# Rotary angles moved from VectorE to GpSimd, the first activation waits for its own input, and x is loaded one step earlier

## What is computed

```python
# first kind: a vector c modulates every sublayer
c_act = silu(c)
for l in range(2):
    mod = (c_act @ ada_w[l] + ada_b[l]).reshape(1, 3, 3, 1024)     # shift, scale, gate of 3 sublayers
    h = modulate(x, norm_pre[l, 0], mod[:, 0, 0], mod[:, 0, 1])    # rms norm, then scale and shift
    x = residual_add(x, swiglu(h, ...), norm_post[l, 0], mod[:, 0, 2], 0.5)
    ...                                                            # token mixer, second feed-forward
# second kind: attention with rotary positions
def rope(x, positions):
    inv_freq = 10000.0 ** (-arange(half) / half)
    ang = positions[..., None] * inv_freq
    cos, sin = cos(ang), sin(ang)
    ...
```

## Time and profile before

| | us |
|---|---|
| median of 3 runs | 2268.48 (2268.31 to 2268.54) |
| the profiled execution | 2269.39 |
| its span, first to last instruction | 2267.8 |
| PE busy | 2219.3 (98%) |
| DVE busy | 1651.8 (73%) |
| ACT busy | 1234.2 (54%) |
| POOL busy | 75.0 (3%) |

### The profile page before, as it was taken

The page is one execution under the profiler, slowest core; times in us unless marked ns, Lnnn a source line. Parts: engine busy times, 40 slices in busy tenths (PEclk is TensorE's granted clock), DMA queues, the critical chain, the costliest instruction groups (busy, mean ns, idle before and its releaser), DMA issues.

```text
span 2267.8 us, 37521 instructions
## 1 busy us (share of the span) xinstructions
PE 2219.3 (98%) x14352; PEld 1985.5 (88%) x14352; DVE 1651.8 (73%) x2339; ACT 1234.2 (54%) x1723; POOL 75.0 (3%) x143
## 2 busy tenths in 40 slices
PE   3999999999999999999999999999999999999998
PEld 3888989988888889899988899889888898898887
DVE  7888777678778888777685667766766666677666
ACT  4445567564445446585564465656644565565444
POOL 0100000000000100000000000000000000000000
PEclk9999999999999999999999999999999999999999
DMA  8877564547666875656555546435555464344553
GB/s 345 311 279 269 188 221 173 196 169 286 250 241 223 294 280 190 225 192 216 193 205 196 192 158 210 137 129 185 185 204 185 153 231 156 131 168 177 203 184 114
DMA packets 79506, 467.27 MB, mean 206 GB/s; under 512 B 10080, under 2 KB 10800, under 8 KB 33168
## 3 DMA queue, kind: packets, MB, share of 16 engines
q1 hardware_dynamic: 58480, 389.38, 47.9%
q0 software_dynamic: 19312, 71.74, 8.8%
q10 hardware_dynamic: 1584, 4.36, 0.5%
HBM read 458.56 MB, written 1.05 MB: 203 GB/s over the span
## 4 chain that ended last, share of the span: by engine, by line
PE 90%; ACT 3%; DVE 2%; issue 1%; DMA 1%; ACTq 1%; DVEq 0%
PE ps L882 21%; PE ps L887 11%; PE ps L552 11%; PE ps L529 10%; PE ps L530 10%; PE ps L531 10%; PE ps L558 5%; PE ps L815 3%; PE ps L822 2%; PE ps L691 1%; PE ps L705 1%; PE ps L738 1%; DVE wlo L1890 1%; DMA raw<-in_ada 1%; ACT whi L1275 1%
## 5 line engine op out<-in xcount | busy, mean ns | idle before, releaser
L1890 DVE TENSOR_TENSOR wlo<-raw,whi 128x2048 fp32r<-128x2048 f32 x360 | 823.6, 2290 | 174.7 <-ACT whi L1275 161.4
L1275 ACT ACTIVATE whi<-raw 128x2048 fp32r<-128x2048 f32 x359 | 686.6, 1914 | 233.8 <-PE ps L531 191.7
L882 PE MATMUL ps<-hx,whi 128*128 128x512 f32 x2112 | 514.4, 391 | 0.1
L882 PEld LDWEIGHTS ps<-hx,whi 128*128 128x128 f32 x2112 | 392.0, 188 | 80.0 <-issue 0.8
L887 PE MATMUL ps<-hx,wlo 128*128 128x256 f32 x2112 | 288.4, 283 | 0.0
L887 PEld LDWEIGHTS ps<-hx,wlo 128*128 128x128 f32 x2112 | 276.7, 191 | 9.9
L552 PE MATMUL ps<-hx,whi 128*128 128x256 f32 x2176 | 276.6, 285 | 0.0
L552 PEld LDWEIGHTS ps<-hx,whi 128*128 128x128 f32 x2176 | 265.6, 191 | 2.9 <-issue 2.4
L529 PE MATMUL ps<-whi,yhi 128*128 128x512 f32 (+1 forms) x560 | 215.6, 385 | 0.0
L530 PE MATMUL ps<-wlo,yhi 128*128 128x512 f32 (+1 forms) x560 | 215.1, 384 | 0.0
L531 PE MATMUL ps<-whi,ylo 128*128 128x512 f32 (+1 forms) x560 | 214.4, 383 | 0.0
(11 more groups left out here) (290 smaller groups left out, 3033.7 us busy)
## 6 DMA issues: line engine op xcount, KB each, us to landing
raw<-in_w SPq DMA_DIRECT2D x360, 1024.0 KB, 4.9
adat<-in_ada POOLq DMA_DIRECT2D x128, 512.0 KB, 4.8
blk<-in_block POOLq DMA_DIRECT2D x2, 926.5 KB, 7.3
raw<-in_ada SPq DMA_DIRECT2D x3, 512.0 KB, 10.4
set_b<-in_ada SPq DMA_DIRECT2D x3, 512.0 KB, 11.9
raw<-in_ada ACTq DMA_DIRECT2D x3, 512.0 KB, 12.7
set_a<-set_b SPq DMA_DIRECT2D x24, 64.0 KB
x<-in_x POOLq DMA_DIRECT2D x1, 1024.0 KB, 10.3
```

The lines of the kernel that those rows point to most:

```text
L882: mm(ps[:, bank + i, :].rearrange("p (a s) -> p a s", a=2), whi[:, slot, k * 256 + i * P:k * 256 + (i + 1) * P], hx[:, :, k, :], start=fir ...
L1275: A(whi[:, slot, :], raw[:, slot, :], ACT.Copy).then_inc(*T.counts("hi_ready"))
L1890: tt(wlo[:, slot, :], raw[:, slot, :], whi[:, slot, :].bitcast(F32), ALU.subtract)\
```

## The change

POOL computes the angles instead of DVE, behind its issue of x and ahead of its wait for `first_used` 16. [...] ACT loads its first table set ahead of its loads of units, activates `c` behind `s_c` alone and waits for `s_pos` afterwards. It no longer takes the sine at the start: that goes into the first feed-forward, ahead of the last chunk, behind `ang_ready`. POOL issues x when unit 1 has landed, not unit 3. Two hooks named `beside` are added to DVE's feed-forward and do nothing by default. The diff, with the angle code of DVE cut to its ends:

```diff
--- before.py
+++ after.py
@@ -1570,7 +1570,7 @@
                 if more:
                     split_ahead()
 
-            def ffn(plain, more=True):
+            def ffn(plain, more=True, sines=False):
                 def gate_up():
                     tile_done()
                     if T.n["sil_ready"] >= 1:
@@ -1589,6 +1589,9 @@
                     for _ in range(2):
                         gate_up()
                         tile_done(False)
+                if sines:
+                    act.wait_ge(sems["ang_ready"], 1)
+                    A(tables2[:, :, :], tables2[:, :, :], ACT.Sin).then_inc(sems["tab_ready"], 1)
                 gate_up()
                 use_ln_exp()
                 last_tile_done(more)
@@ -1600,13 +1603,12 @@
             act.dma_start(pos_in, posin.partition_broadcast(P)).then_inc(s_pos, 16)
             act.dma_start(const[:, N_MATRICES:], const_in[:, N_MATRICES:]).then_inc(s_pos, 16)
             act.dma_start(const[:, 0:N_MATRICES], const_in[:, 0:N_MATRICES]).then_inc(s_const, 16)
+            act.preload_act_table_set("silu_and_others")
             for i in (0, 1, 3, 5, 7, 9, 11):
                 act.dma_start(first_ada[i], ada[i]).then_inc(s_first[i], 16)
-            act.wait_ge(s_pos, 32)
             act.wait_ge(s_c, 16)
             A(cact[:, :], cact[:, :], ACT.Silu).then_inc(*T.counts("c_ready"))
-            act.wait_ge(*T.next("ang_ready"))
-            A(tables2[:, :, :], tables2[:, :, :], ACT.Sin).then_inc(*T.counts("tab_ready"))
+            act.wait_ge(s_pos, 32)
             use_ln_exp()
             split_high()
             act.wait_ge(s_x, 16)
@@ -1630,7 +1632,7 @@
                     if layer == 0:
                         act.wait_ge(sems["raw_full1"], 16)
                         A(whi[:, 1, :], raw[:, 1, :], ACT.Copy).then_inc(sems["hi_ready"], 1)
-                    ffn(False)
+                    ffn(False, sines=layer == 0)
                     sublayer_begin(modf[:, 1, 8:16], modf[:, 1, 0:8])
                     for i in range(4):
                         tile_done()
@@ -2204,7 +2206,7 @@
                 if more:
                     split_low()
 
-            def ffn(ada_units=0, after=lambda: None, more=True, plain=False, own_gate=None):
+            def ffn(ada_units=0, after=lambda: None, more=True, plain=False, own_gate=None, beside=lambda i: None):
 
 
                 chunk = [0]
@@ -2267,8 +2269,10 @@
                 if own_gate is not None:
                     unit(2, own_gate)
                 ada(0)
+                beside(0)
                 gate_up(own_gate if own_gate is None else own_gate + 3)
                 tile_done(False)
+                beside(1)
                 if own_gate is not None:
                     unit(2, own_gate + 3)
                 ada(1)
@@ -2288,31 +2292,6 @@
                 sublayer_end(plain, ALONG, ("bank_done", "bank_done", "bank_done", "tile_used"), more)
 
 
-            v.wait_ge(s_pos, 32)
-            posf, ang, kf = bufA[:, 0, 0:S], bufA[:, 1, 0:S], bufB[:, 0, 0:S]
-            nc.vector.tensor_copy(posf, pos_in[:, :])
-            v.drain()
-            ts(ang, posf, c("invf"), None, ALU.mult)
-            v.drain()
-            for i, quarter in enumerate((0.25, 0.0)):
...
-                last = ts(r, r, -3.1415925, 3.1415925, ALU.max, ALU.min)
-            last.then_inc(*T.counts("ang_ready"))
             v.wait_ge(*T.next("c_ready"))
             for i in range(16):
                 v.wait_ge(s_first[i], 16)
@@ -2447,7 +2426,7 @@
                     ffn(ada_units=2 if more else 0, after=last_gate, own_gate=18)
 
 
-            v.wait_ge(*T.next("tab_ready"))
+            v.wait_ge(sems["tab_ready"], 1)
             cos2, sin2 = tables2[:, 0, :], tables2[:, 1, :]
             for layer in range(DEPTH):
                 with T.layer(LAYER2):
@@ -2629,8 +2608,40 @@
             g.memset(idle[:, :].bitcast(F32), 1.0).then_inc(s_idle, 1)
             g.dma_start(par1_all[:, :], par1_in).then_inc(s_load, 16)
             g.dma_start(norms2_all[:, :], norms2_in[:, 0:16 * DEPTH]).then_inc(s_load, 16)
-            g.wait_ge(s_first[3], 16)
+            g.wait_ge(s_first[1], 16)
             g.dma_start(x[:, :, :], xin).then_inc(s_x, 16)
+            posf, ang, kf = bufA[:, 0, 0:S], bufA[:, 1, 0:S], bufB[:, 0, 0:S]
+            gts_, gtt, term = nc.gpsimd.tensor_scalar, nc.gpsimd.tensor_tensor, bufB[:, 1, 0:S]
+            g.wait_ge(s_pos, 32)
+            nc.gpsimd.tensor_copy(posf, pos_in[:, :])
+            g.drain()
+            gts_(ang, posf, c("invf"), None, ALU.mult)
+            g.drain()
+            for i, quarter in enumerate((0.25, 0.0)):
+                gts_(kf, ang, 1.0 / (2 * math.pi), quarter, ALU.mult, ALU.add)
+                g.drain()
+                gts_(kf, kf, ROUND, ROUND, ALU.add, ALU.subtract)
+                g.drain()
+                r = tables2[:, i, :]
+                gts_(term, kf, -PI2[0], None, ALU.mult)
+                g.drain()
+                gtt(r, ang, term, ALU.add)
+                g.drain()
+                gts_(term, kf, -PI2[1], None, ALU.mult)
+                g.drain()
+                gtt(r, r, term, ALU.add)
+                g.drain()
+                gts_(term, kf, -PI2[2], None, ALU.mult)
+                g.drain()
+                gtt(r, r, term, ALU.add)
+                g.drain()
+                if i == 0:
+                    gts_(r, r, math.pi / 2, None, ALU.add)
+                else:
+                    gts_(r, r, c("rsign"), None, ALU.mult)
+                g.drain()
+                last = gts_(r, r, -3.1415925, 3.1415925, ALU.max, ALU.min)
+            last.then_inc(sems["ang_ready"], 1)
             g.wait_ge(sems["first_used"], 16)
             for i in range(2):
                 g.dma_start(adat[:, i, :], ada[16 + i]).then_inc(sems[f"ada_full{i}"], 16)
```

## The result

| | kernel before | changed kernel |
|---|---|---|
| median, us (5 runs each, side by side) | 2268.54 (2268.31 to 2269.27) | 2279.01 (2278.14 to 2280.12) |
| the profiled execution, us | 2269.39 | 2279.01 |
| its span, us | 2267.8 | 2277.4 |
| POOL busy, us | 75.0 | 104.1 |

The ratio is 1.0047 (95% interval 1.0035 to 1.0058): the change costs 10.5 us. The forecast was 2271.2, with a range that ended at 2276.0. Of the 10.5 us, 9.6 stand between the two profiled executions; the other 0.9 is that the profiled execution of before lay that much above its median.

The account below looks back on a forecast made before the run. PE's main matmuls bound the kernel, so only the start and pace of the first ones count. Angles, activation, sine and x 0, then +1.6, +0.5, +0.6 = +2.7 us on 2268.5 gave 2271.2, range 2267.5 to 2276.

Parts of the forecast that it names:

- the 1 us allowed: Sign of error for DVE's reduction of unit 9: the forecast is wrong if that unit lands over 1 us off 29.4.
- The table load: ACT's table load, now ahead of its seven unit loads: taken to cost zero, upper bound 1.28 us on F.
- F: End of DVE's 16th reduction, 37.69 before; forecast 39.3, 1.6 us late, bounds 0 and 5.3.
- The three terms: Ahead of and at the first main matmuls: +1.6 us at F, +0.5 at the first piece, +0.6 for PE's clock.
- The sine: ACT's sine (0.63 us), moved into the first feed-forward, where ACT idles 3.56 us: cost zero.
- the walk: Step-by-step timing of POOL's angles beside DVE's reductions: nine operations through when unit 9 starts, at 29.6.
- part four: The 22 angle operations on POOL: POOL and DVE hold each other up, F 1.6 us late, first piece 0.5 us more.
- rival (b): POOL's refill of adat becomes DVE's wait; at 1.8 us per operation 10 more, +12.7, 2281; chance 0.12.
- Part one: Angles off DVE at the start: the 6.5 us freed are worth nothing to F, since data landings decide.

## Why the prediction was wrong

**Right, with their sizes.** The first reduction was at 13.66 (13.3 forecast); unit 9 at 28.83 (29.6, so earlier, within the 1 us allowed); x landed by 26.29 (26.4) and the transposes ended at 35.44 (35.6). The activation of c came at 6.59 instead of 7.7, which changed nothing. The table load didn't hold up ACT's unit loads: it ran from 2.35 to 3.63 while the issues went on, the last at 6.08 against 5.82 in the earlier trace rows. The reductions beside POOL took 1.34 to 1.74 us instead of 1.22. From unit 9 to F it was 9.9 us where 9.7 was forecast and 8.3 was measured before; F was 38.7 (39.3), since unit 9 came early, and the first main matmul 41.29 (41.8). The three terms were +1.6, +0.5 and +0.6; by the rows they are +0.99, +0.49 and +0.76, together 2.2 where 2.7 was forecast. The sine started at 206.37 with ACT's next split waiting for PE anyway: zero, as forecast. Of the hold between reductions and POOL, which the Trainium skill states on its page "SBUF — State Buffer", section "Who interferes with whom", these rows are now an example: 1.22 us became 1.34 to 1.74. Its "GPSIMD Engine Reference", section 3.1, had given me an estimate of 0.56 us for a two-input operation of 256 columns; alone, beside an idle DVE, one took 0.74 here, and the measurement decides.

**The step that failed** is the walk in part four, "Starting at 16.7, nine are through when unit 9 starts", and with it rival (b)'s "POOL's angles end near 44.5". One was through, not nine. The walk had "plus a drain" inside its 0.4 us between two operations, and put the drain behind POOL's own load of x at nothing, without a reason. The angles ended at 56.2, 11.7 us later. Of that 8.9 us are this drain (9.06 less the usual 0.15). The other 2.8 are the price of an operation: where there was no gap, 22 of them took from 16.23 to 46.66, 1.38 us each, against 1.26 in the walk. Between reductions the walk's pace was right, one POOL operation to each reduction; it was wrong for those left over behind the reductions, of which two met DVE's splits of 2.3 to 2.5 us and took 2.70 and 2.39.

**What followed was rival (b)**, word for word as far as its mechanism goes, but by another cause: it needed 1.8 us for each operation, and had an end near 56 that way. Its price was 56 + 7.2 - 53.2 = 10 us. The refill landed in 3.7 us instead of 7.2, so that the same sum gives 6.7; the rows show 4.8 of waiting and 1.7 of slow matmuls behind it, which I had not thought of. With the first part's 2.2 that makes 8.8. That (b)'s 2281 lies so near the measured 2279 is in part luck: its cause, its wait and its clock were each off.

**What the bounds should have been.** The trace of before has no drain of POOL's behind a load of POOL's, so nothing in it priced one. But the walk put 20 drains behind a load of 10.32 us. With that load as the upper bound for the first of them, the angles would have ended between 44.5 and 44.5 + 10.3 = 54.8. The point from which (b) decides was 46. A forecast whose margin is 1.5 us on one side and which has an unpriced 10 us on the other gives that rival more than 0.12.

**Part one was nearly right, for a reason that matters more:** the angles in front of DVE cost the 16th reduction 0.55 us, of the 6.5 us that they take. The run without any angles is no faster than the kernel before, while taking the units as they land, with the angles left where they were, brings the 16th reduction forward by 1.7 us.

**Left open.** The last 0.8 us between the two traces, which come up after the first feed-forward; whether the half microsecond of the angles can be won with PE kept busy; what decides after which short gap PE is slow; and why the medians of the two kernels in landing order agree while their traces differ by 0.96 us.

## What to carry to other kernels

Before work is moved to an idle engine, list what that engine has queued behind it and by when each is needed: here the engine was 3% busy, and its few loads decided the result. POOL, issuing loads and computing with drains between the steps, paid at the next drain for each of its own loads in flight, so either let another queue issue them or keep such computing off POOL. Taking only one of the loads away did not help here: the run that let SP issue the refill was as slow, since unit 18 was then late. And work that stands in front of a wait for data costs little (0.55 of 6.5 us here); look first at the order in which the data land.

## What the runs showed of the hardware

- **A drain on POOL waits for POOL's own loads.** 9.06, 6.78, 8.83 and 3.51 us of idleness, each ending within 0.5 us behind the landing of the load issued before it; 0.15 us, once 0.46, without a load; two conversions without a drain ran right beside the load. A drain on ACT did not wait for ACT's own load (30.77 against a landing near 31.8).
- **POOL and DVE hold each other, on POOL's side too.** In the changed kernel one angle operation of 256 columns, behind the first conversion, took 0.74 to 1.07 us beside an idle DVE, 0.81 to 2.70 beside reductions, and 2.70 and 2.39 beside splits of 2.47 and 2.29. The reductions took 1.34 to 1.74 instead of 1.22.
- **The same load on another queue:** x took 9.9 us on POOL's queue and 16.5 on ACT's, issued within 0.2 us of the same moment, with ACT's unit loads ahead of it.
- **PE came back slower from some short idleness, not from all.** After 0.84 us without work, matmuls that take 0.40 us took 0.63, at a granted clock of 0.51, the lower of the two levels (1.2 GHz); after 4.63 us a group of 16 took 5.53 instead of 3.82, at 0.68 in the mean (64.0 to 69.4). Without a gap the first one took 0.39. But behind 0.98 us without work eight fillers took 1.22, at 0.98, and behind 0.82 us, where ACT issues x, the first matmul took 0.50 and the next 0.40. The printed clock doesn't always show it: the changed kernel's slow pieces from 41 to 44 stand under 1.00.
